# First block's second attention: waves ordered by group, transposed exponentials in two halves, outputs a step later, query splits between the waves

## The reference

```python
# per block of 128 queries
s = einsum('tghd,cgd->tghc', qt, k_cmp) * scale          # compressed keys: 31 of them
p_cmp = masked_softmax(s, cmp_last <= t)
o_cmp = einsum('tghc,cgd->tghd', p_cmp, v_cmp)
...                                                       # all 8 key blocks are chosen (top 16 of 8)
s = einsum('tghd,tgkd->tghk', qt, ksel) * scale           # branch 0, causal
o_slc = einsum('tghk,tgkd->tghd', masked_softmax(s, kpos <= t), vsel)
s = einsum('tghd,kgd->tghk', qt, kw) * scale              # branch 1, window of 512, causal
o_win = einsum('tghk,kgd->tghd', masked_softmax(s, mw), vw)
o = gt[0] * o_cmp + gt[1] * o_slc + gt[2] * o_win
```

## Time and profile before

| | us |
|---|---|
| median of 3 runs | 3318.38 |
| lowest, highest | 3315.14, 3320.82 |
| the profiled execution's own time | 3305.71 |
| span of its records | 3303.6 |
| mean granted TensorE clock (1 is 2.4 GHz) | 0.951 |
| PE, PEld busy | 3069.8, 2591.9 |
| DVE, ACT, POOL busy | 1627.9, 1166.7, 232.4 |

### The profile page before, as it was taken

How to read it: one execution, slowest core, us unless ns; L and a number is a source line. 1 busy time by engine, 2 the same in 40 slices (tenths; PEclk the granted TensorE clock), 3 DMA queues, 4 the chain that set the end, 5 groups by cost and what they waited for, 6 DMA issues and landing times.

```text
span 3303.6 us, 39487 instructions
## 1 busy us (share of the span) xinstructions
PE 3069.8 (93%) x15764; PEld 2591.9 (78%) x15764; DVE 1627.9 (49%) x2706; ACT 1166.7 (35%) x1952; POOL 232.4 (7%) x186
## 2 busy tenths in 40 slices
PE   7899999899888999999888989999999989999998
PEld 5678787687777788878667887888888779878887
DVE  6756666645565666662244664222222455443333
ACT  3632223424554322241244653211112345432222
POOL 2010001000353000010000101000000100010001
PEclk9899999968788999999989999999999989899999
DMA  4235544331001354442000001211221110023331
GB/s 144 80 105 160 163 156 134 96 118 44 1 1 45 115 166 157 155 147 67 26 20 12 24 25 52 71 61 62 63 65 58 51 52 1 14 83 97 95 102 65
DMA packets 75127, 260.09 MB, mean 79 GB/s; under 512 B 8129, under 2 KB 10689, under 8 KB 74817
## 3 DMA queue, kind: packets, MB, share of 16 engines
q1 hardware_dynamic: 74944, 257.57, 24.4%
HBM read 255.44 MB, written 2.10 MB: 78 GB/s over the span
## 4 chain that ended last, share of the span: by engine, by line
PE 58%; ACT 4%; DVE 4%; issue 2%; DMA 0%; DVEq 0%; POOL 0%; SPq 0%; ACTq 0%
PE PS L493 56%; PE PS L1234 2%; DVE SM L2162 1%; ACT TMP L1241 0%; PE PS L1268 0%; ACT PB L1241 0%; ACT PB L1225 0%; ACT TMP L1225 0%; ACT WH L418 0%; DVE PS L1983 0%; ACT Q L1163 0%; DVE NKL L1907 0%; DVE TMP L606 0%; DVE WL L424 0%; DVE SM L1855 0%
## 5 line engine op out<-in xcount | busy, mean ns | idle before, releaser
L493 PE MATMUL PS<-UH,WH 128*128 128x512 f32 x2296 | 872.2, 380 | 68.6 <-DVE UL L619 19.4
L493 PE MATMUL PS<-UL,WH 128*128 128x512 f32 x2296 | 860.0, 375 | 0.0
L493 PE MATMUL PS<-UH,WL 128*128 128x512 f32 x2296 | 856.6, 373 | 0.0
L418 ACT ACTIVATE WH<-RAW 128x1024 fp32r<-128x1024 f32 (+1 forms) x367 | 379.6, 1037 | 916.8 <-PE PS L493 595.1
L424 DVE TENSOR_TENSOR WL<-RAW,WH 128x1024 fp32r<-128x1024 f32 (+1 forms) x367 | 445.8, 1217 | 386.8 <-ACT WH L418 376.6
L493 PEld LDWEIGHTS PS<-UH,WH 128*128 128x128 f32 x2296 | 440.4, 192 | 161.0 <-DVE WL L424 27.9
L493 PEld LDWEIGHTS PS<-UL,WH 128*128 128x128 f32 x2296 | 440.2, 192 | 78.5 <-issue 5.6
L493 PEld LDWEIGHTS PS<-UH,WL 128*128 128x128 f32 x2296 | 438.5, 191 | 77.3
L493 PE MATMUL PS<-HH,WH 128*128 128x512 f32 x1008 | 369.0, 366 | 2.6 <-DVE HL L2032 2.6
L493 PE MATMUL PS<-HL,WH 128*128 128x512 f32 x1008 | 369.3, 366 | 0.0
L493 PE MATMUL PS<-HH,WL 128*128 128x512 f32 x1008 | 367.4, 365 | 0.0
(11 more groups left out here) (320 smaller groups left out, 4230.5 us busy)
## 6 DMA issues: line engine op xcount, KB each, us to landing
RAW<-in_mod_w SPq DMA_DIRECT2D x96, 512.0 KB, 3.6
RAW<-in_f_in SPq DMA_DIRECT2D x88, 512.0 KB, 3.6
RAW<-in_g_in SPq DMA_DIRECT2D x88, 512.0 KB, 3.5
RAW<-in_f_out SPq DMA_DIRECT2D x32, 448.0 KB, 4.1
RAW<-in_g_out SPq DMA_DIRECT2D x32, 448.0 KB, 3.2
RAW<-in_a_in SPq DMA_DIRECT2D x16, 512.0 KB, 3.7
RAW<-in_f_out SPq DMA_DIRECT2D x16, 512.0 KB, 4.1
RAW<-in_g_out SPq DMA_DIRECT2D x16, 512.0 KB, 3.5
```

The costliest lines, as they stand in the source:

```text
L418: act.e.activation(hi, raw, ACT.Copy).then_inc(wh.step(n, i), 1)
L493: return pe.e.matmul(out, l, r, start=start, stop=stop)
```

## The change

- The waves are ordered by group: for each g a compressed wave, and then q = 0 to 3. A compressed wave now holds the 4 heads of its group for all 4 query blocks; it is again 32 matmuls of 32 columns.
- The place "across" is used as two halves of 512 columns, a ring of its own ("half"). Transposes, the copy to `PTH` and the remainder `PTL` come in halves (512 and 512, or 512 and 256 columns), each with its own semaphore steps.
- TensorE's order in a step becomes scores of wave s, outputs of wave s - 5, transposes of wave s - 3. `BOT`, `SUM`, and the high and low parts of the result come one step later.
- Of the query splits only group 0's four stand ahead of the first step; those of group s stand in steps 1 to 3, on VectorE between the maximum and the reciprocal, on ScalarE between the exponentials and the copy.
- `VC` holds all four groups' values on each of the four partition ranges: the copies are 256 wide instead of 64.
- The mask of blind queries is applied in each compressed wave, to the four columns of query block 0.

```diff
-         "score": [("lin", 0), ("lin", 1)], "across": [("lin", 2)]},
-        tallies, None if book is None else book["left"])
+         "score": [("lin", 0), ("lin", 1)], "across": [("lin", 2)], "half": [("half", 0), ("half", 1)]},
+        {("lin", 2): [("half", 0), ("half", 1)]}, tallies, None if book is None else book["left"])
...
-                x, v = TMP[:, 0, 0:256].rearrange("p (g d) -> p g d", g=4), TMP[:, 1, 512:576]
-                for g in range(4):
-                    act.wait_ge(dve_c.after("v"), dve_c.after("vc zero"))
-                    act.e.activation(v[32 * g:32 * g + 31, :], x[0:31, g, :], ACT.Copy).then_inc(act_c.step("v", g), 1)
+                x, v = TMP[:, 0, 0:256].rearrange("p (g d) -> p g d", g=4), TMP[:, 1, 512:768].rearrange("p (g d) -> p g d", g=4)
+                act.wait_ge(dve_c.after("v"), dve_c.after("vc zero"))
+                for i in range(4):
+                    act.e.activation(v[32 * i:32 * i + 31, :, :], x[0:31, :, :], ACT.Copy).then_inc(act_c.step("v", i), 1)
                 act.wait_ge(act_c.after("v", 3))
-                act.e.activation(VC[:, 0:64], v, ACT.Copy).then_inc(act_c.step("vc"), 1)
+                act.e.activation(VC[:, :, 0:64], v, ACT.Copy).then_inc(act_c.step("vc"), 1)
...
-        for q in range(4):
-            waves.append(Wave(q, None, [], 0, [], False, False))
-            L = 128 * (q + 1)
-            for g in range(4):
-                heads = range(4 * g, 4 * g + 4)
+        for g in range(4):
+            waves.append(Wave(g, None, [], 0, [], False, False))
+            heads = range(4 * g, 4 * g + 4)
+            for q in range(4):
...
+    def wave_halves(n):
+
+        N = 512 if NW[n].q is None else 128 * sum(len(heads) for _, _, heads in NW[n].tiles)
+        return [(a, min(a + 512, N)) for a in range(0, N, 512)]
...
+            if s < len(NW):
+                nsa_scores(pe, s)
+            if 0 <= s - 5 < len(NW) and NW[s - 5].q is not None:
+                nsa_outputs(pe, s - 5)
+            if 0 <= s - 3 < len(NW):
+                nsa_transposes(pe, s - 3)
...
+    def nsa_transposes(pe, n):
...
+        pe.wait_ge(scaled.after("nsa", n))
+        for i, (a, z) in enumerate(wave_halves(n)):
+            o = psum.enter("half", "across", "nsa", n, i)
+            pe.wait_ge(*psum.clear("across", "nsa", n, i))
+            for j in range((z - a) // 128):
+                last = pe.e.transpose(o[:, 128 * j:128 * j + 128], columns_of[a // 128 + j], con("ident"))
+            last.then_inc(across.step("nsa", n, i), 1)
...
+    def nsa_split_vector(dve, g):
+        for i in (2 * g, 2 * g + 1):
+            for j in range(2):
+                query_low(dve, "nsa", i, j, ...)
...
     def nsa_vector(dve):
-        split_queries("nsa", QRAW, None, "dve", dve)
+        nsa_split_vector(dve, 0)
...
-                dve.wait_ge(evac.after("nsa", n))
-                hi, lo = (PCH, PCL) if NW[n].g is None else (PTH[PLACE[n] % 2], PTL[PLACE[n] % 2])
-                dve.e.tensor_tensor(lo[:, 0:N], o[:, 0:N], hi[:, 0:N].bitcast(F32), ALU.subtract).then_inc(copy.step("nsa", n), 1)
-                psum.leave(("across", "nsa", n), copy)
+                hi, lo = (PCH, PCL) if NW[n].q is None else (PTH[PLACE[n] % 2], PTL[PLACE[n] % 2])
+                for i, (a, z) in enumerate(wave_halves(n)):
+                    dve.wait_ge(evac.after("nsa", n, i))
+                    dve.e.tensor_tensor(lo[:, a:z], psum.at["across", "nsa", n, i][:, 0:z - a], hi[:, a:z].bitcast(F32),
+                                        ALU.subtract).then_inc(copy.step("nsa", n, i), 1)
+                    psum.leave(("across", "nsa", n, i), copy)
...
+            if 0 < s < 4:
+                nsa_split_vector(dve, s)
             n = s - 1
...
-            n = s - 5
+            n = s - 6
             if 0 <= n < len(NW) and NW[n].last:
```

More of the change, by code:

```diff
@@ L78, in enter @@
         self.turn[ring] += 1
-        self.before[key] = self.holder.get(place)
-        self.holder[place] = key
+        parts = self.halves.get(place, [place])
+        self.before[key] = {self.holder[part] for part in parts if part in self.holder}
+        for part in parts:
+            self.holder[part] = key
         self.at[key] = self.aps[place]
@@ new lines, in nsa_outputs @@
+    def nsa_outputs(pe, n):
+        g, q, _, _, tiles, first, final = NW[n]
+        if first:
+            psum.enter("aux", "out", g, q)
+            pe.wait_ge(*psum.clear("out", g, q))
+        o = psum.at["out", g, q]
+        hi, lo = PTH[PLACE[n] % 2], PTL[PLACE[n] % 2]
+        pe.wait_ge(dve_c.after("vv", 1))
+        c = 0
+        for br, k, heads in tiles:
+            N, a = 128 * len(heads), 128 * (heads[0] - 4 * g)
+            v = VV[:, k, 4 * br + g, :]
+            pe.wait_ge(copy.after("nsa", n, c // 512))
+            mm(pe, o[:, a:a + N], v, hi[:, c:c + N], first and br == 0 and k == 0, False)
+            last = mm(pe, o[:, a:a + N], v, lo[:, c:c + N], False, False)
+            c += N
+        if final:
+            r = slice(32 * q, 32 * q + 32)
+            pe.wait_ge(copy.after("nsa", CMP[g], 0), dve_c.after("vc"))
+            mm(pe, o[:, 0:512], VC[r, g, :], PCH[r, :], False, False)
+            last = mm(pe, o[:, 0:512], VC[r, g, :], PCL[r, :], False, True)
+        last.then_inc(outp.step("nsa", n), 1)
@@ L1437, in nsa_scalar @@
-                psum.leave(("across", "nsa", n), evac)
-            n = s - 5
-            if 0 <= n < len(NW) and NW[n].last:
-                q, g = NW[n].q, NW[n].g
-                act.wait_ge(outp.after("nsa", n), *([fin.after("nsa", *before_group(q, g), 1)] if (q, g) > (0, 0) else []))
-                act.e.activation(BOT[LO, :], psum.at["out", q, g][HI, :], ACT.Copy).then_inc(act_o.step("nsa", q, g, "bottom"), 1)
+                for i, (a, z) in enumerate(wave_halves(n)):
+                    act.wait_ge(across.after("nsa", n, i))
+                    if NW[n].q is None:
+                        act.wait_ge(*([outp.after("nsa", n - 1)] if n else []))
+                        hi = PCH
+                    else:
+                        old, hi = earlier(n, 2), PTH[PLACE[n] % 2]
+                        act.wait_ge(*([] if old is None else [outp.after("nsa", old)]))
+                    act.e.activation(hi[:, a:z], psum.at["across", "nsa", n, i][:, 0:z - a], ACT.Copy).then_inc(evac.step("nsa", n, i), 1)
+                    psum.leave(("across", "nsa", n, i), evac)
@@ L1452, in nsa_vector @@
+                act.e.activation(BOT[LO, :], psum.at["out", g, q][HI, :], ACT.Copy).then_inc(act_o.step("nsa", g, q, "bottom"), 1)
+            n = s - 7
+            if 0 <= n < len(NW) and NW[n].last:
+                g, q = NW[n].g, NW[n].q
+                act.wait_ge(fin.after("nsa", g, q, 1))
+                act.e.activation(Q2[:, q, 4 * g:4 * g + 2, :], SUM.rearrange("p (t n) -> p t n", t=2), ACT.Copy).then_inc(act_o.step("nsa", g, q, "hi"), 1)
     def nsa_vector(dve):
-        split_queries("nsa", QRAW, None, "dve", dve)
+        nsa_split_vector(dve, 0)
```

208 lines of the change are left out of this document (89 added, 119 removed).

## The result

The changed kernel took 3289.89 us (median of 4 runs, 3283.38 to 3291.99), the kernel before beside it 3316.93 (4 runs, 3315.14 to 3320.82): a ratio of 0.9914, with a 95% interval of 0.9896 to 0.9931. Run again, beside 23 runs of the kernel before, it gave 0.9908 [0.9894, 0.9922]. A ratio here is taken over the undisturbed executions, so it can differ a little from the quotient of the medians, and three far longer executions stay out of it (4494.81 us of the kernel before, 4831.73 and 7463.23 of two variants).

A forecast was written before the change was run, and what follows sets the result against it. Slow TensorE bounds the entry, a ring of waits the rest. Group 0 to 855.4, three groups 157.5 to 1012.9, draining to 1029.8 against 1043.65: 13.8 us gained, 13.4 taken off 3318.4, 3305 us; range 3290 to 3321.

The forecast's parts named there:

- the ring of the one place: Steady 1024-wide waves: transposes, ScalarE's copy and VectorE's subtraction take turns at one place; 3.53 us before, about 3.1 forecast.
- steps 6 to 11 of group 0: TensorE's six steps from 831.0 us, priced 24.4 us in all, ending at 855.4.
- the draining: Stage end after 1012.9 us: three steps 2.6 + 4.0 + 2.8, 6 for the last outputs, 1.5 for low clock.
- The low clock: First of TensorE's steps 6 to 11 in group 0: clock still low, outputs 128x512 costing 2.6 us; step priced 6.0.
- Steady and closing steps: Later steps of each group: 2.9 us where VectorE sets it, 3.4 with compressed matmuls, 3.9 or 4.0 with SUM.
- the chain between ScalarE and VectorE: In a transition between groups, priced by TensorE's work alone; named as what would break the sum, no size given.
- Queries between the waves: Stage entry: TensorE's compressed scores end 2.4 us earlier, but first low half at 825.2 against 825.39, nothing gained there.
- Closings: Last wave of a group and query: TensorE finds its place free some 1.3 us late, against 1.9 before.
- Compressed values: ScalarE copies 256 wide, 0.41 against 0.27 us each: +0.8 us on the path, between 0 and 1.5.
- Rival 2: Clock comes back within the transition and holds: 48.5 us a group, 24 to 28 us gained, 3292; chance 0.18.
- Rival 3: Gain given back in latency by VectorE's and ScalarE's extra work: steady waves near 3.3 us, 3318 overall; chance 0.20.
- Rival 4: Transition's low clock lasts through query-1 and first query-2 steps: 64 us a group, 3339 overall, slower; chance 0.12.

The follow-up runs named there:

- second execution: The changed kernel run again unedited, beside 23 runs of the kernel before: 3286.13 us, ratio 0.9908, stage 216.6 us.

## Why the prediction was half right

The direction and the cause were right: the ring of the one place bound the stage, and the halves break it. The size was half.

**The step that failed** is the term "steps 6 to 11 of group 0, the clock low in the first: 6.0 + 4.4 + 3.4 + 4.4 + 3.1 + 3.1 = 24.4, to 855.4". It took 19.1 us. I priced TensorE's steps, so I read them on TensorE, each from its first score to that of the next:

```profile
835.40 0.42 PE L500 MATMUL PS<-KHw,Q 128*128 128x384 f32 x1
...
838.92 0.42 PE L500 MATMUL PS<-KHw,Q 128*128 128x384 f32 x1
...
841.42 0.48 PE L500 MATMUL PS<-KHs,Q 128*128 128x512 f32 x1
...
845.35 0.48 PE L500 MATMUL PS<-KHs,Q 128*128 128x512 f32 x1
...
854.52 0.26 PE L500 MATMUL PS<-KCH,Q 128*128 128x32 f32 x1
```

These are the starts of steps 6, 7, 8, 9 and 12; they give 3.5, 2.5 and 3.9 us for steps 6 to 8, and 9.2 for 9 to 11. To compare times with the forecast I take 5.2 us off, since the stage began that much later. The low half of wave 0 then came at 825.7, forecast 826.0, and step 5 ended at 830.2, forecast 831.0: up to there the sum held. The 12.0 us that the stage was shorter than forecast (17.4 in the second execution, see the rivals) are 0.8 up to there, 5.3 in steps 6 to 11, 3.8 in the three groups (51.4, 51.2 and 51.1 us, where I had taken 52.5), and 2.1 in the draining (14.8 for 16.9), where the 1.5 for a low clock were not needed: it was 0.99 there.

Two wrong prices make the 5.3.
- *The low clock*, 2.5 us. I had it last through step 6, at 6.0. The windows show 0.50 up to 834.5 and 0.99 from there, and the step took 3.5.
- *Steady and closing steps*, 2.8 us. Steps 7 to 11 took 15.6 where I had 18.4. I priced them from VectorE's 3.1 for a 1024-wide wave. For a step that is 1024 wide in both its parts 3.1 was fair: the kernel before with halves does 2.93, TensorE-bound, and I had TensorE at 3.0. But a step on VectorE joins the remainder of one wave and the maximum of the wave four later, and in a group most of those pairs are 768 with 1024. Such a step takes 2.14: the two pieces of a 768-wide remainder take 1.02 together (of a 1024-wide one 1.29, where I had twice 0.69, 1.38), and the 0.4 us of waiting that I added is not there, since the first half has been copied while VectorE took the last maximum. The closing steps on VectorE, 4.3 and 4.7, cost what I had said or more (4.0 and 4.4).

Within a group the errors mostly cancel. On TensorE the first four steps, the transition, took 22.8, 23.7 and 23.6 us for the 24.5 in my 52.5, and the remaining eight 28.6, 27.5 and 27.5 for 28. But in the eight the first step took 5.4 for 3.4, and the last five 15.6 for 17.2. The 5.4 stand where ScalarE's copy of the compressed wave waits for the last outputs of the group before, VectorE waits for the copy, and TensorE for VectorE. That is the chain between ScalarE and VectorE that I had named as what would break the sum; it is worth about 2 us a group, and had the other sign to the errors above. That the eight came out right is luck.

**What belongs to which part** I had not asked sharply enough, and it is the larger lesson. I priced the order by group as the frame in which the halves gain, and gave it the end of SUM's wait for POOL's Q, 11.9 us. By the experiments the order alone gains nothing (0.9996), and the halves alone everything (0.9920). The wait of 11.9 does go away, but the stage is no shorter; SUM waits 26.2 us for BOT there instead of 18.3, and where the rest went was not looked for. With halves in both, the order by group, the split queries and the later outputs together make no difference that shows (0.9920 without them, 0.9914 and 0.9908 with them).
- *Queries between the waves.* I said that nothing is gained up to the first low half, 825.2 against 825.39; it was 825.7, right. But I compared with the kernel before and not with the same order with its splits ahead, which is 6 us or more earlier there and, with BOT first in both, 7.0 at the end. This part costs some 7 us (4 to 8 by the ratios) inside a change that gains 27.
- *Closings.* I forecast the detour at 1.3 us. It is mostly avoidable: BOT ahead of the copies takes 6 to 11 us off the stage, 0.4 to 0.7 a closing.
- *Compressed values.* Some 1 us was expected. The stage began 5.2 us later; but so it did in the kernel before with halves, at 801.1, which has not this edit, and kernels that have it began between 796.8 and 805.6. The scatter is larger than the cost, which stays open.

**The rivals.** Rival 2 forecast "24 to 28 us gained", and 27 came, but that is luck and not its mechanism: the clock was at 0.50 to 0.52 in all three transitions of the profiled execution. In the second execution its mechanism was there once. The same stretch of the third transition, whose compressed mask came at 960.87 and 961.27, first in the changed kernel as profiled first:

```profile
960.00:965.00 5.00, 5.00 (x27) 4.12 (x26) 2.45 (x5) 0.68 (x2) 1.98 (x3) 0.63 0.00 0
965.00:970.00 5.00, 5.00 (x24) 5.00 (x25) 1.15 (x3) 1.03 (x2) 0.33 (x1) 0.50 0.00 0
```

and in the second execution:

```profile
960.00:965.00 5.00, 5.00 (x42) 4.49 (x41) 3.18 (x6) 1.61 (x3) 1.99 (x3) 1.00 0.00 0
965.00:970.00 5.00, 5.00 (x46) 5.00 (x45) 2.96 (x6) 2.10 (x6) 1.81 (x3) 1.00 0.00 0
```

46 matmuls in the second five microseconds instead of 24, and all of the 5.4 us by which the two stages differ (26.7 against 21.2 us from the last steady step to the next compressed remainder). So one low transition costs some 5.4 us by this one pair, near the 6.6 that I had between my two group prices. The Trainium skill, page "TensorE: Matmul & The Clock Gate", section "What's actually happening", says that the clock follows how busy the engine has been. The trace agrees only in part: TensorE was busy 5.00 of 5.00 us in all four windows above, at 0.63 and 0.50 in the one execution and at 1.00 in the other.
Rival 3, the gain given back in latency, fell: the steady steps have no such wait. Rival 4 fell: no low stretch of a transition in the changed kernel was longer than some 14 us.

**The list of signs.** Stage end: 1028 forecast, 1023.05 with a later start. First compressed scores from 799 to 806: 804.08. Pitch 3.1: 2.14 in mixed steps. Transposes waiting for PTL "under 10": 10.4. No SUM wait for POOL's Q over 2: right. Low clock once per transition, 8 to 12 us: once per transition it was, for 10.5, 13.0 and 13.5.

## What to carry to other kernels

Where an in-order pipeline turns on one buffer, count its ring from the release back to the release, and halve the buffer before anything is reordered: here early filling and early freeing were worth 10 to 17 us each, and the order of the waves nothing. Price a step of a software pipeline by the pieces that meet in it, which belong to different iterations and may have different sizes. And compare each part of a change with the change without it, not only with the kernel before: a part that costs some 4 to 8 us hid inside a gain of 27, and the kernel without it and with one copy moved ahead is at 0.9853.

## What I had not expected of the hardware

- Pieces of one subtraction cost less than their sum: one 128x512 piece takes 0.69 us, two back to back 1.29, and 128x512 with 128x256 1.02. My price for the halves on VectorE was too high by 0.09 us a 1024-wide wave.
- The same program, in the same place, ran one transition at 0.50 and at 1.00 in two executions, with TensorE busy throughout in both. 5.4 us of the stage depend on it.
- The stretches outside the stage, in which nothing differs but the place of some work, vary by 12 us between the profiles (3060 to 3072, and 3055.8 once), and by 6 between the two of the changed kernel. A gain of ten microseconds can't be read from two spans, but it can from the stage.
